# A two-layer decoder step on one core: first normalisation in token-major form, and a last output stage with one PSUM bank for each half tile

## The reference, cut to what matters

```python
def layer_norm(x, g, b):
    mu = jnp.mean(x, -1, keepdims=True)
    var = jnp.mean(jnp.square(x - mu), -1, keepdims=True)
    return (x - mu) * lax.rsqrt(var + LN_EPS) * g + b

xp = layer_norm(concat([meta, x_prompt]), emb_ln_g, emb_ln_b)   # the first norm
...
for l in range(2):
    x = layer_norm(ALPHA * x + token_mixer(x), ln1_g[l], ln1_b[l])
    x = layer_norm(ALPHA * x + conv_ffn(x), ln2_g[l], ln2_b[l])  # for l = 1: the last norm
```

## Time and profile before

| | |
|---|---|
| median of 3 runs | 1586.23 us (1585.19 to 1592.24) |
| profiled execution, own time | 1596.57 us |
| its span, first to last instruction | 1594.3 us |
| mean granted TensorE clock | 0.965 |
| PE busy | 1505.8 us, 94% of the span |
| VectorE, ScalarE busy | 923.2 us (58%), 686.4 us (43%) |

### The profile page before, as it was taken

How to read it: one execution, slowest core, us unless ns; L and a number is a source line. 1 busy time by engine, 2 the same in 40 slices (tenths; PEclk the granted TensorE clock), 3 DMA queues, 4 the chain that set the end, 5 groups by cost and what they waited for, 6 DMA issues and landing times.

```text
span 1594.3 us, 30590 instructions
## 1 busy us (share of the span) xinstructions
PE 1505.8 (94%) x12047; PEld 1221.0 (77%) x12047; DVE 923.2 (58%) x1499; ACT 686.4 (43%) x1067; POOL 89.1 (6%) x86
## 2 busy tenths in 40 slices
PE   3899999999999999999989999999999999999995
PEld 2677878777788888878767887877777888887874
DVE  5767775546755555533476777555585555553334
ACT  4655552343743434322365555333264343432224
POOL 0011112110000000000001111111000000000000
PEclk7999999999999999999999999999899999999998
DMA  7222233221223222232333322321212323222321
GB/s 210 71 82 81 81 86 103 83 87 62 80 80 105 79 94 90 72 85 86 107 93 86 82 81 81 108 82 54 88 61 80 104 80 105 79 80 75 96 73 57
DMA packets 175042, 138.19 MB, mean 87 GB/s; under 512 B 5064, under 2 KB 169192, under 8 KB 174776
## 3 DMA queue, kind: packets, MB, share of 16 engines
q1 hardware_dynamic: 168192, 113.46, 23.8%
q0 software_dynamic: 5408, 18.60, 4.2%
q10 hardware_dynamic: 1372, 5.16, 0.9%
HBM read 125.12 MB, written 12.07 MB: 86 GB/s over the span
## 4 chain that ended last, share of the span: by engine, by line
PE 75%; DVE 10%; ACT 8%; DVEq 3%; issue 2%; ACTq 1%; DMA 1%; SPq 0%
PE ACC L561 62%; ACT X L973 2%; ACT XH L972 1%; PE OT L705 1%; PE SCR L735 1%; DVE Fb L1460 1%; PE OT L757 1%; DVE WL L1380 1%; PE SCR L618 1%; PE SCR L806 1%; DVE X L1430 1%; ACT WH L946 1%; PE SCR L561 1%; PE OT L561 1%; DVE B L1466 1%
## 5 line engine op out<-in xcount | busy, mean ns | idle before, releaser
L561 PE MATMUL ACC<-XH,WH 128*128 128x280 f16 x2304 | 483.6, 288 | 8.4 <-DVE XL L1435 6.6
L561 PE MATMUL ACC<-XL,WH 128*128 128x280 f16 x2304 | 483.1, 287 | 0.0
L561 PE MATMUL ACC<-XH,WL 128*128 128x280 f16 x2304 | 482.7, 287 | 0.0
L1380 DVE SCALAR_TENSOR_TENSOR WL<-stage,WH 128x2048 f16<-128x2048 f32 (+1 forms) x108 | 228.8, 2119 | 128.0 <-ACT WH L946 121.7
L561 PEld LDWEIGHTS ACC<-XH,WH 128*128 128x128 f16 x2304 | 227.8, 101 | 70.6 <-DVE XL L1435 8.4
L561 PEld LDWEIGHTS ACC<-XL,WH 128*128 128x128 f16 x2304 | 228.8, 99 | 54.4 <-issue 0.9
L561 PEld LDWEIGHTS ACC<-XH,WL 128*128 128x128 f16 x2304 | 229.1, 99 | 53.4
L946 ACT ACTIVATE WH<-stage 128x2048 f16<-128x2048 f32 (+1 forms) x108 | 190.5, 1764 | 98.4 <-PE ACC L561 71.9
L561 PE MATMUL ACC<-shared,WH 128*128 128x280 f16 x1320 | 214.7, 283 | 2.0 <-issue 2.0
L561 PEld LDWEIGHTS ACC<-shared,WH 128*128 128x128 f16 x1320 | 128.8, 98 | 31.2 <-issue 3.1
L561 PE MATMUL ACC<-shared,WL 128*128 128x280 f16 x660 | 139.8, 283 | 0.0
(11 more groups left out here) (262 smaller groups left out, 2004.0 us busy)
## 6 DMA issues: line engine op xcount, KB each, us to landing
stage<-in_w_in_dram SPq DMA_DIRECT2D x64, 512.0 KB, 5.3
stage<-in_w_a_dram SPq DMA_DIRECT2D x44, 512.0 KB, 4.3
stage<-in_w_b_dram SPq DMA_DIRECT2D x44, 512.0 KB, 4.4
stage<-in_w_down_dram SPq DMA_DIRECT2D x32, 384.0 KB, 3.5
stage<-in_w_down_dram SPq DMA_DIRECT2D x32, 320.0 KB, 3.9
out_dram<-shared POOLq DMA_DIRECT2D x16, 512.0 KB, 3.9
stage<-in_w_o_dram SPq DMA_DIRECT2D x16, 512.0 KB, 3.9
shared<-in_state_ret_dram POOLq DMA_DIRECT2D x8, 512.0 KB, 4.6
```

Of the source, the lines that this page charges most:

```text
L561: last = mm(dst(h), lhs, x[:, xk + k, tokens(h)], start=begin, stop=end)
L1380: stt(out=wl[:, 0:width], in0=stage[:, s, 0:width], scalar=W_SCALE, in1=wh[:, 0:width], op0=ALU.mult, op1=ALU.subtract).then_inc(w_lo[s], 1)
```

## The change

The opening. The token tiles are loaded one by one with a semaphore each. The norm is now made token-major, on `XT` itself: `token_sums` (VectorE) takes two `bn_stats` over 512 columns each and a `bn_aggr`, which give each token's mean and variance; `token_deviation` (ScalarE) makes 1/deviation as a 128x1 column; `token_norm` (VectorE) applies both in one instruction over 128x1024. TensorE then transposes normalised tokens: for the left half tiles 0 to 2 into eight PSUM places (`left_bank`), one for each row k; for the right half tiles 2 to 4 row by row into four banks used twice (`right_bank`), in pieces between the matmuls of the left half. Gain and bias are applied as the rows leave PSUM: left rows by `opening_rows` (VectorE, then XH by `left_high` on ScalarE), right rows by `right_rows` (ScalarE, XH and X). No `norm_stats` is left in the opening. The right half's 96 matmuls start behind one wait, for all eight counts of `x_ready`. The gains and biases come in 10 loads ahead of the 4 of the convolution weights, ScalarE's table load stands first in its program, and the load of the large tables behind `token_deviation(4)`.

The end. Each half tile has a bank of its own (`out_bank`). Tile 0 is transposed ahead of `norm_stats`, tile 1 directly behind it. The right half is transposed pair by pair as its rows are scaled, for tiles 2, 3 and 4 at once; VectorE scales the rows of pair 3 itself (L2070 of the changed kernel), and ScalarE issues all six stores behind its last copy.

```diff
+            def transpose_right(m):
+                pe.wait_ge(x_ready, (2, 2, 3, 4, 5, 5, 6, 6)[m])
+                pe.wait_ge(token_rows, TT5)
+                for i in range(LEFT_TILES - 1, TT5):
+                    n, at_ = P if i < 4 else R5, i * P - RIGHT0
+                    last = nc.tensor.transpose(right_bank[m][:, at_:at_ + n], XT[0:n, i, m * P:(m + 1) * P], ident[0:n, 0:n])
...
+                transpose_left()
+                pe.wait_ge(w_lo[0], 2)
+                for k in range(KT):
+                    if k % 2 == 0:
+                        pe.wait_ge(x_ready, k // 2 + 1)
+                    one(k, pairs[0], 0)
+                    for m in {4: (0, 1), 5: (2,), 7: (3,)}.get(k, ()):
+                        transpose_right(m)
+                pe.wait_ge(w_lo[1], 2)
+                for k in range(KT):
+                    one(k, pairs[1], 0)
+                    for m in {2: (4, 5), 5: (6, 7)}.get(k, ()):
+                        transpose_right(m)
+                pe.wait_ge(x_ready, 2 * PAIRS)
+                for pair in pairs:
+                    for k in range(KT):
+                        one(k, pair, 1)
...
+            def right_rows(pair):
+                for m in (2 * pair, 2 * pair + 1):
+                    act.wait_ge(row_full, KT + m + 1)
+                    src = right_bank[m][:, HALF - RIGHT0:T - RIGHT0]
+                    g, b = (norm_column(0, o, m) for o in range(2))
+                    f(XH[:, m, tokens(1)], src, ACT.Identity, scale=g, bias=b)
+                    last = f(X[:, m, tokens(1)], src, ACT.Identity, scale=g, bias=b)
+                last.then_inc(ln_out, 1)
...
+            def token_sums(i):
                 n = P if i < 4 else R5
+                dve.wait_ge(x_in[i], 32 if i in (0, 4) else 16)
+                for h in range(2):
+                    nc.vector.bn_stats(SUM6[0:n, 12 * i + 6 * h:12 * i + 6 * h + 6], XT[0:n, i, 512 * h:512 * h + 512])
+                dve.drain()
+                nc.vector.bn_aggr(MEAN_VAR[0:n, 2 * i:2 * i + 2], SUM6[0:n, 12 * i:12 * i + 12])
+                dve.drain().then_inc(token_var, 1)
+
+            def token_norm(i):
+                n = P if i < 4 else R5
+                dve.wait_ge(token_rstd, i + 1)
+                ts(XT[0:n, i, :], XT[0:n, i, :], MEAN_VAR[0:n, 2 * i:2 * i + 1], RSD[0:n, i:i + 1], ALU.subtract, ALU.mult).then_inc(token_rows, 1)
+
+            def opening_rows(pair):
+                for m in (2 * pair, 2 * pair + 1):
+                    dve.wait_ge(row_full, m + 1)
+                    ts(X[:, m, tokens(0)], left_bank[m][:, 0:HALF], norm_column(0, 0, m), norm_column(0, 1, m), ALU.mult, ALU.add)
+                dve.drain().then_inc(left_rows, 1)
```

```diff
             scr = Scratch(base(DEPTH))
+            pe.wait_ge(ln_out, left + 2)
+            out_rows(0, 0, range(0, 4))
+            pe.wait_ge(ln_out, left + PAIRS)
+            out_rows(0, 1, range(4, 8))
             norm_stats(4 * DEPTH + 1, 1, reads0(DEPTH), scr.bank[1])
...
+            out_rows(1, 0, range(0, 4))
+            out_rows(1, 1, range(4, 8))
...
+            for pair in range(PAIRS):
...
+                if pair < PAIRS - 1:
+                    pe.wait_ge(ln_out, right + pair + 1)
+                else:
+                    pe.wait_ge(last_rows, 1)
+                if pair % 2 == 0:
+                    pe.wait_ge((out_ready, out_right)[pair // 2], 1)
+                for i in (2, 3, 4):
+                    out_rows(i, pair // 2, (2 * pair, 2 * pair + 1))
...
+            norm_mean(4 * DEPTH + 1, 1, ot0(DEPTH) + 1)
+            left_columns(0)
+            norm_rstd(4 * DEPTH + 1, 2 * DEPTH, 1)
+            left_columns(1)
+            for pair in range(PAIRS - 1):
+                norm_rows(4 * DEPTH + 1, 2 * DEPTH, 1, pair, False)
+            for i in range(2, TT5):
+                left_columns(i)
+            for i in range(TT5):
+                store(i)
```

More of the change, by code:

```diff
@@ new lines, in transpose_left @@
+            def transpose_left():
+                pe.wait_ge(consts_in, 16)
+                for i in range(LEFT_TILES):
+                    if i == LEFT_TILES - 1:
+                        pe.wait_ge(norms_in, 16 * N_NORM_DMAS)
+                        nc.tensor.transpose(norms_bank, rows[0:ROWS2, 2, :], ident[0:ROWS2, 0:ROWS2]).then_inc(norms_full, 1)
+                    pe.wait_ge(token_rows, i + 1)
+                    for m in range(KT):
+                        if i == LEFT_TILES - 1 and m == KT - 1:
+                            pe.wait_ge(norms_ready, 1)
+                        last = nc.tensor.transpose(left_bank[m][:, i * P:(i + 1) * P], XT[:, i, m * P:(m + 1) * P], ident)
+                        if i == LEFT_TILES - 1:
+                            last.then_inc(row_full, 1)
@@ new lines, in transpose_right @@
+            def transpose_right(m):
[4 more added lines that the diff above has]
+                    last = nc.tensor.transpose(right_bank[m][:, at_:at_ + n], XT[0:n, i, m * P:(m + 1) * P], ident[0:n, 0:n])
+                if m == KT - 1:
+                    last.then_inc(ot_full, 2)
+                    pe.wait_ge(params_in, 16 * N_CONV_DMAS)
+                    for b in range(DEPTH):
+                        last = nc.tensor.transpose(conv_bank[:, b * ROWS01:(b + 1) * ROWS01], rows[0:ROWS01, b, :], ident[0:ROWS01, 0:ROWS01])
+                last.then_inc(row_full, 1)
@@ new lines, in opening_units, with one @@
+            def opening_units():
+                pairs = ((1, (acc(0), acc(1))), (2, (lambda h: OT[:, h, 0:HALF], lambda h: SCR[:, h, 0:HALF])))
+                def one(k, pair, h):
+                    for c in range(2):
+                        last = products(pair[1][c], pair[0], 2 * P, c * P, lambda _: k, XH, XL, k, 1, k == 0, k == KT - 1, (h,))
+                        if h == 1 and k == KT - 1:
+                            last.then_inc(acc_full, 1)
+                transpose_left()
[15 more added lines that the diff above has]
+                        one(k, pair, 1)
@@ new lines, in _ @@
+            for i in range(LEFT_TILES):
+                token_deviation(i)
+            act.wait_ge(norms_full, 1)
+            f(par[:, 2 * P:2 * P + ROWS2], norms_bank, ACT.Copy)
+            act.drain().then_inc(norms_ready, 1)
+            split_hi(0, 0, (acc_full, 1), slot=1)
+            for i in range(LEFT_TILES, TT5):
+                token_deviation(i)
+            act.dma_start(tab[:, first_tables:n_const], consts[:, first_tables:n_const]).then_inc(tables_in, 16)
+            for pair in range(PAIRS):
+                left_high(pair)
+                if pair == 1:
+                    split_hi(1, 0, (acc_full, 1), slot=2)
@@ L1768, in _ @@
+            token_norm(4)
+            opening_rows(3)
             norm_low(0, 0, 2)
```

272 lines of the change are left out of this document (118 added, 154 removed).

## The result

Over nine runs of each kernel the changed kernel takes 1578.75 us (1571.98 to 1582.70), the kernel before 1593.51 us (1585.19 to 1605.66). The ratio is 0.9903, with a 95% interval of 0.9875 to 0.9932: 1.0% faster. The forecast step of 16.2 us, from 1586.2 to 1570.0, is a ratio of 0.9898 and lies in that interval; the forecast time of 1570.0 does not hold, and 1578.75 is 0.75 us above the range. The interval of the ratio is wide: of 1593.5 us it is 10.8 to 19.9 us. The profiled execution takes 1582.7 us with a span of 1581.0, against 1596.57 and 1594.3 before: 13.9 and 13.3 us less.

What follows compares the result with a forecast made beforehand. TensorE, busy 94% of the span, was taken to bound the body, with VectorE's work delaying the opening. Opening 10.5 plus end 5.7 gave 16.2 us, taken from the runs' median of 1586.2: 1570.0 us, range 1562 to 1578.

Steps and rivals of the forecast that it cites:

- I take the same 16.2 from the runs' median of 1586.2: Whole kernel: the gain summed on the profiled span, 16.2 us, taken off the runs' median of 1586.2, giving 1570.0 us.
- My 2 us for the spread of medians: Whole kernel: 2 us allowed for the spread of medians in the likeliest case's own range.
- the likeliest case: Whole kernel: 1570 us, own range 1564 to 1575, opening gaining 8.4 to 12.5 and end 3.2 to 7.7; chance 0.78.
- the slow start of the block: Opening, right half's 96 matmuls: after a 5.5 us stand, the first 14 run at half pace, costing 1.6 us.
- the last issue 0.3 us behind the last copy: End: VectorE's copies end at 1583.4 and the last store is issued at 1583.7 instead of 1591.3.
- 401 GB/s for all of it: End: all stores, 2.23 MB, move at 401 GB/s in 5.6 us, so the end gains 5.7 us.
- Rival 4: End: stores queue at 274 GB/s, nothing else wrong, giving 1572.5 us; counted in the likeliest case, no separate chance.
- The body: Between the two ends: the same 1498 us as before, from the opening's end to the last residual.
- Rival 1: Opening gains half or less, from stage 0 no earlier or dearer `bn_stats`; 1572 to 1578 us; chance 0.14.
- Rival 2: Opening: TensorE stays at 1.2 GHz, so the opening loses 5 us; result 1585.5, no change; chance 0.05.
- Rival 3: Opening, right half's single wait: the kernel is slower if it opens after 71 instead of 46.9; chance 0.03.
- The rule against small loads: Opening's token loads: by a 1 MiB minimum, tiles 3 and 4 come 1.2 us late, 1571.2 instead of 1570.0.

Runs made afterwards that it cites:

- the first four experiments: The kernels e1_opening, e2_end, e4_tables_early and e3_gate, compared with 29 runs of the kernel before; ratios 0.9938, 0.9952, 0.9953 and 0.987.
- the last two: e6_stores, and the changed kernel with the edits of e6_stores and e3_gate together, compared with 12 runs of the kernel before; ratios 0.99 and 0.9833.
- e1_opening: The changed opening with the end of the kernel before; ratio to the kernel before 0.9938 (0.9912 to 0.9964).
- e4_tables_early: The changed kernel with the large tables' load issued early again, as in the kernel before; ratio to the kernel before 0.9953 (0.993 to 0.9975).
- e3_gate: The changed kernel with the right half's last two XL pairs ahead of VectorE's next low split, plus one TensorE wait; ratio to the kernel before 0.987.
- e6_stores: The changed kernel with stores of tiles 0, 1 and 3 issued by SyncE once each tile is ready; ratio to the kernel before 0.99 (0.9864 to 0.9936).
- e2_end: The opening of the kernel before with the changed end; ratio to the kernel before 0.9952 (0.9926 to 0.9977).

## Why the prediction was right or wrong

**The step that failed** is "I take the same 16.2 from the runs' median of 1586.2". Three runs do not fix this kernel's level (the time around which its executions scatter). With nine runs its median is 1593.51; the 29 runs beside the first four experiments have 1591.92, the 12 beside the last two 1594.53. Two of the first three lay at the lower edge of a spread of 21 us (1584.45 to 1605.66 over all of them). The profiled execution, at 1596.57, stood 10 us above the median of three, and I set it aside; it is only 3 us above the median of nine. With 16.2 taken from 1593.5 the forecast would have been 1577.3, and the range around it would have held 1578.75. My 2 us for the spread of medians was the mis-sized term: the base measured 7.3 us higher. (By its own terms the likeliest case reached to 1576.6, not 1575: 1586.2 - 8.4 - 3.2 + 2.) Of the 8.75 us between 1570.0 and 1578.75 the base is 7.3 and the step the other 1.4 (the medians lie 14.8 us apart, forecast 16.2).

The step itself is confirmed less well than the ratio makes it look. The two ends measured in the profiled executions give 9.4 + 4.65 = 14.05 us, about 2 us less than the forecast sum; that the ratio gives 15.5 (0.97% of 1593.5) is within its wide interval and partly luck.

The spread goes with the granted clock: of the 29 runs, the 14 with a mean clock of 0.973 or less have a median of 1596.3 us, the nine between 1591.9, the six with 0.977 or more 1589.3. What sets a run's clock no run here shows.

**The opening: mechanism right, 9.4 us instead of 10.5.** The steps in us from the start of the program:

| step | forecast | measured |
|---|---|---|
| tokens of tile 0 there | 7.1 | 6.2 |
| left transposes done | 17.4 | 15.7 |
| WH of stage 0 starts | 17.7 | 16.7 |
| first matmul | 22.7 | 21.7 |
| last right row in PSUM | 39.9 | 39.3 |
| ScalarE starts on that row | 39.9 | 39.8 |
| WL done | 45.4 | 45.8 |
| block of 96 opens | 46.9 | 47.1 |

The sums of one tile took about 1.6 us, as forecast. The first matmul was early by a microsecond, and nothing came of it, since the block hangs on the right rows. The term that was off is the slow start of the block: I charged 14 matmuls at half pace, 1.6 us. The timeline of the changed kernel has the pace change here:

```profile
51.53 0.40 PE L606 MATMUL ACC<-XL,WH 128*128 128x280 f16 x1
51.77 0.29 PE L606 MATMUL ACC<-XH,WL 128*128 128x280 f16 x1
```

That is 20 matmuls at 0.233 us, 4.65 us where full pace takes 2.4: 2.3 us. In `e1_opening` it was about 15 (from 46.77 on, full pace from about 50.3), in `e4_tables_early` 14 (52.32 to 55.5). This number differs between executions whose stand is the same 6.04 or 6.05 us, so the opening's gain has a spread of about 1 us of its own: 9.4 here, 10.3 in `e1_opening`. `e3_gate` settles what the slow start comes from, for without the stand there is none.

**The end: mechanism right, 4.65 us instead of 5.7.** Up to the copies the sum holds. Counted from the last residual, the first store is issued at 12.8 (forecast 12.5) and VectorE's last copy ends at 15.1 (forecast 14.9). (One sum on the way is off: twelve transposes at 1.11 us for four are 3.3 us, to 1582.4, where the prediction has 1581.9.) But the last store is issued at 17.0, forecast 15.2. The prediction put the last issue 0.3 us behind the last copy, as if an issue cost the same with other stores in flight as without; the six took 0.35, 0.38, 0.82, 1.19, 1.12 and 1.20 us. The second mis-sized term is the queue's time. The stretches of the changed kernel's end (columns as in the earlier trace rows) show why 401 GB/s for all of it was too high:

```profile
1573.00:1574.00 1.00, 0.49 (x3) 0.02 (x1) 0.88 (x2) 0.00 (x0) 0.00 (x0) 0.50 0.58 164
1574.00:1575.00 1.00, 0.00 (x0) 0.00 (x0) 0.86 (x2) 0.00 (x0) 0.00 (x0) 0.94 0.97 279
1575.00:1576.00 1.00, 0.00 (x0) 0.00 (x0) 0.00 (x0) 0.00 (x0) 0.00 (x0) 1.00 0.98 393
1576.00:1577.00 1.00, 0.00 (x0) 0.00 (x0) 0.00 (x0) 0.00 (x0) 0.00 (x0) 1.00 1.07 434
...
1579.00:1580.00 1.00, 0.00 (x0) 0.00 (x0) 0.00 (x0) 0.00 (x0) 0.00 (x0) 0.50 0.59 160
```

The full rate is there only from 1575 to 1579. With its start and its tail the queue needs about 7 us for the 2.23 MB instead of 5.6. The last store, on record as issued at 1576.89, ends the span 4.1 us later; in `e1_opening`, with one large and one small store in flight in front of it instead of three and one, 2.6 us. The landing of the 512 KB stores tells the same, issue to landing, in the changed kernel and then in the kernel before:

```profile
out_dram<-shared ACTq DMA_DIRECT2D x3, 512.0 KB, 4.7
```

```profile
out_dram<-shared ACTq DMA_DIRECT2D x3, 512.0 KB, 2.6
```

The new end does not use the DMA engines between 1567.2, when tile 0 is ready, and 1572.6. `e6_stores` starts there and gets 1.9 us of it back. Rival 4 (274 GB/s, a gain of 3.2 us) lies 1.5 us from the 4.65, the forecast 1.1: the truth is between the two.

**The body.** Forecast 1498, measured 1499.1. Over the eight profiled executions it ranges from 1488.6 (`e2_end`, `e4_tables_early`) to 1499.1. One of these two has the old opening and the other the changed one, both with the changed end, which the changed kernel has too; so it does not follow the edits. The traces show where such time goes. One stretch of the body with the same 213 matmuls, in the changed kernel and then in `e4_tables_early` (columns as in the earlier trace rows):

```profile
309.60:343.40 33.80, 32.01 (x213) 24.52 (x211) 15.58 (x26) 15.65 (x30) 3.71 (x4) 0.90 0.21 63
```

```profile
314.05:344.43 30.38, 28.61 (x213) 22.83 (x211) 15.26 (x26) 15.62 (x30) 3.69 (x3) 1.00 0.23 70
```

At a mean granted clock of 0.90 it takes 3.4 us longer than at 1.00. Over the whole body the granted clock stands at 0.50 for 65 us in the changed kernel, 55 in `e4_tables_early` and 44 in `e2_end`. At half pace, 10 us more of it cost at most 5 us and 20 us more at most 10, so this accounts for about all of the difference to `e2_end` and for half of that to `e4_tables_early`. Why the clock falls in one execution and not in another stays open. It is part of the spread above, and the reason why the profiled difference of 13.3 us (9.4 + 4.65 - 0.75) and the ratio's 15.5 us need not agree.

**The rivals.** Rival 1 fell on both counts: stage 0 came early, and `e4_tables_early` shows that the tables had held it up; the statistics took 0.64 us each (two in 1.29), below my 0.69. Rival 2 fell: TensorE ran at full pace from 24.6 to the stand and again from 51.8. Rival 3, the block's wait, was the right place to look, but it opened at 47.1, far from the 71 from which it would have decided; its price was 8.4 us of a gain that could have been had.

**The rule against small loads.** By it the prediction estimated tiles 3 and 4 late by 1.2 us. In the trace the statistics of tiles 3 and 4 wait for no load: tile 3's start at 13.60, directly behind the scaling of tiles 1 and 2, and tile 4's at 15.29, behind tile 3's. The Trainium skill, "DMA: Bandwidth & Descriptors", section "Rules for kernel authors", asks for at least 1 MiB a DMA for the highest bandwidth; here three loads of 512 KB in the place of one of 1536 KB cost nothing that the trace shows: the last of the three had landed at 12.1, the single load at 12.4, with the DMA engines full meanwhile (share 1.06 in 5 to 10 us). The 2 us that the prediction took with it stand in another section of that page of the Trainium skill, "Anatomy of one DMA — SWDGE (gpsimd) path", as a fit for DMAs issued from GpSimd; these loads are issued by SyncE.

## What to carry to other kernels

Look behind a new single wait for everything that the releasing engine has to do first: here two instructions of 0.7 us each stood behind a whole weight split, and moving them ahead of it was worth 8.4 us of the opening, nearly as much as the rewritten opening's 9.4. When an opening starts earlier, ask which transfer made room for it; half of this one hung on a moved load of tables that nobody needed yet. And take a forecast of one per cent from a ratio, or from as many runs as the spread asks for: a median of three runs was 7 us off, more than three times the error of the whole sum (about 2 us).

## What the runs showed of the hardware that I had not expected

- A store's issue is not a constant. On ScalarE's queue it took 0.34 to 0.38 us with at most one earlier store of that queue not yet landed, 0.45 to 0.96 us with two (0.45 in `e1_opening`, 0.82 in the changed kernel, 0.96 in `e6_stores`) and 1.12 to 1.21 us with three or more. On SyncE's queue in `e6_stores`, where the stores were 2 us and more apart, it took 0.34 to 0.38 us. An engine that issues stores back to back stands for that time.
- TensorE's clock. TensorE stood from about 41.1 to 47.1. The granted clock of the changed kernel was still 1.00 (2.4 GHz) at the start of that stand, fell to 0.50 (1.2 GHz) within it, and was back only after 20 matmuls:

```profile
43.00:44.00 1.00, 0.00 (x0) 0.00 (x0) 0.53 (x1) 0.44 (x1) 0.00 (x0) 1.00 0.67 61
...
45.00:46.00 1.00, 0.00 (x0) 0.00 (x0) 1.00 (x2) 0.00 (x0) 0.00 (x0) 0.50 0.79 246
...
51.00:52.00 1.00, 1.00 (x7) 0.65 (x5) 0.00 (x0) 0.00 (x0) 0.00 (x0) 0.62 0.12 27
```

- The left half's transposes ran 0.21 us apart until about 14.1 (two from 13.71, the next at 14.14) and 0.11 apart from there (14.83, 14.94), with nothing but transposes on the engine (rows of the changed kernel's timeline):

```profile
13.71 0.63 PE L535 MATMUL ACC<-tab,shared 128*128 128x128 f32 x2
14.14 0.32 PE L535 MATMUL OT<-tab,shared 128*128 128x128 f32 x1
...
14.83 0.27 PE L535 MATMUL OT<-tab,shared 128*128 128x128 f32 x1
14.94 0.38 PE L535 MATMUL ACC<-tab,shared 128*128 128x128 f32 x2
```

  The granted clock reads 1.00 for all of 10 to 16 us, so in the first microseconds of this kernel that column does not tell the pace, and the spacing of instructions has to be read instead. Why, no run here shows. The Trainium skill, "TensorE: Matmul & The Clock Gate", "Part 4: PE-mode transpose", says that a transpose does not count as busy in the same way as a matmul and that the full clock does not engage for it; this spacing speaks against it, as the earlier trace rows did.
- The time of one kernel on a single core moves by more than 1% between executions (1584.45 to 1605.66 us for the kernel before), with mean granted clocks of 0.965 to 0.981.
